# Spreading the adaLN gate's weight units evenly between the query projections of a hybrid attention kernel

## The reference

```python
def mixer_layer(x, c, pos, past, w_ada, b_ada, ln_gain, w_in, ...):
    mod = einsum('bd,de->be', silu(c), w_ada) + b_ada
    shift, scale, gate = split(mod, 3)
    h = rmsnorm(x, ln_gain) * (1 + scale) + shift
    q_a, ckv, krope, g_a, q_b, k_b, v_b, q_i, k_i, w_i, g_b = split(h @ w_in)
    # group A: latent attention over ckv, krope            -> o_a
    # group B: score = sum_g relu(q_i . k_i) * w_i ; top-k keys;
    #          softmax attention over them with a relative bias  -> o_b
    y = concat([rmsnorm(o_a) * silu(g_a), rmsnorm(o_b) * silu(g_b)])
    return x + gate * (y @ w_out)        # then a last rmsnorm
```

## Time and profile before

| | us |
|---|---|
| median of 3 runs | 999.13 (996.65 to 999.48) |
| the profiled execution's own time | 999.13 |
| its span in the profile | 997.3 |
| TensorE busy | 930.2 (93%) |
| TensorE's weight loads | 800.4 (80%) |
| VectorE busy | 428.0 (43%) |
| ScalarE busy | 340.7 (34%) |
| GpSimd busy | 116.9 (12%) |

### The profile page before, as it was taken

The page is one execution under the profiler, slowest core; times in us unless marked ns, Lnnn a source line. Parts: engine busy times, 40 slices in busy tenths (PEclk is TensorE's granted clock), DMA queues, the critical chain, the costliest instruction groups (busy, mean ns, idle before and its releaser), DMA issues.

```text
span 997.3 us, 14192 instructions
## 1 busy us (share of the span) xinstructions
PE 930.2 (93%) x5707; PEld 800.4 (80%) x5707; DVE 428.0 (43%) x882; ACT 340.7 (34%) x629; POOL 116.9 (12%) x189
## 2 busy tenths in 40 slices
PE   3798799999999999999999999998989999979996
PEld 0366478899999688888999889787978899868885
DVE  2221343336432145333333462349345566846462
ACT  2322342334311234223321542333134335632341
POOL 1000003102100000011103100102011101820000
PEclk9899899999999999999999999999999999999999
DMA  8999948665433234464324767547567753883423
GB/s 316 387 345 349 361 160 258 162 151 153 136 126 94 73 96 131 126 207 143 116 78 122 237 223 235 182 133 239 176 194 229 244 163 101 299 264 106 127 64 126
DMA packets 129537, 185.37 MB, mean 186 GB/s; under 512 B 30048, under 2 KB 79896, under 8 KB 128320
## 3 DMA queue, kind: packets, MB, share of 16 engines
q1 hardware_dynamic: 115744, 138.71, 44.3%
q0 software_dynamic: 13728, 45.76, 13.9%
HBM read 173.84 MB, written 12.69 MB: 187 GB/s over the span
## 4 chain that ended last, share of the span: by engine, by line
PE 80%; DMA 6%; DVE 5%; ACT 4%; issue 2%; SPq 2%; POOL 1%; DVEq 0%; ACTq 0%; POOLq 0%
PE proj L1736 30%; PE proj L1725 26%; DMA gl_b<-gate_scratch 3%; PE proj L1752 2%; DMA araw<-in_w_ada 2%; PE bankO L1709 2%; DVE w_lo L1276 2%; SPq L694 2%; PE bankO L1833 1%; PE bankO L1842 1%; PE proj L1709 1%; PE bankS L1752 1%; PE bankS L1959 1%; ACT w_hi L938 1%; DMA raw<-in_w_in 1%
## 5 line engine op out<-in xcount | busy, mean ns | idle before, releaser
L1276 DVE TENSOR_TENSOR w_lo<-raw,w_hi 128x1024 fp32r<-128x1024 f32 (+2 forms) x164 | 200.3, 1226 | 239.6 <-ACT w_hi L938 238.9
L938 ACT ACTIVATE w_hi<-raw 128x1024 fp32r<-128x1024 f32 (+2 forms) x164 | 167.7, 1026 | 191.0 <-PE proj L1725 101.5
L1736 PE MATMUL proj<-hT_hi,w_hi 128*128 128x384 f32 x640 | 222.2, 347 | 3.9 <-DVE w_lo L1276 2.8
L1736 PE MATMUL proj<-hT_hi,w_lo 128*128 128x384 f32 x640 | 215.1, 336 | 0.0
L1736 PE MATMUL proj<-hT_lo,w_hi 128*128 128x384 f32 x640 | 214.8, 336 | 0.0
L1725 PE MATMUL proj<-w_hi,hT_hi 128*128 128x512 f32 (+2 forms) x464 | 181.3, 391 | 16.0 <-DVE w_lo L1276 14.0
L1725 PE MATMUL proj<-w_hi,hT_lo 128*128 128x512 f32 (+2 forms) x464 | 176.3, 380 | 0.0
L1725 PE MATMUL proj<-w_lo,hT_hi 128*128 128x512 f32 (+2 forms) x464 | 176.0, 379 | 0.0
L1736 PEld LDWEIGHTS proj<-hT_hi,w_hi 128*128 128x128 f32 x640 | 121.0, 189 | 11.5 <-issue 7.2
L1736 PEld LDWEIGHTS proj<-hT_lo,w_hi 128*128 128x128 f32 x640 | 120.9, 189 | 0.5 <-issue 0.2
L1736 PEld LDWEIGHTS proj<-hT_hi,w_lo 128*128 128x128 f32 x640 | 120.6, 189 | 0.0
(11 more groups left out here) (350 smaller groups left out, 1043.5 us busy)
## 6 DMA issues: line engine op xcount, KB each, us to landing
raw<-in_w_in SPq DMA_DIRECT2D x104, 512.0 KB, 3.7
araw<-in_w_ada SPq DMA_DIRECT2D x128, 256.0 KB, 7.6
raw<-in_w_ada SPq DMA_DIRECT2D x32, 512.0 KB, 4.7
raw<-in_w_out SPq DMA_DIRECT2D x32, 512.0 KB, 3.9
raw<-in_w_in SPq DMA_DIRECT2D x32, 256.0 KB, 3.2
raw<-in_w_in SPq DMA_DIRECT2D x32, 128.0 KB, 2.6
wuk<-in_w_uk POOLq DMA_DIRECT2D x16, 256.0 KB, 3.8
kload<-in_cache_dsa_k POOLq DMA_DIRECT2D x8, 512.0 KB, 6.4
```

Of the source, the lines that this page charges most:

```text
L938: return nc.scalar.activation(out, in_, func, scale=scale, **kw)
L1276: V.tensor_tensor(w_lo[:, SLOT[u], 0:w], raw_of(u)[:, 0:w], high(u)[:, 0:w].bitcast(F32), ALU.subtract).then_inc(lo_ready, 1)
L1736: ins = mm(banks[blk][:, 0:TOK], w[:, n, cols], a[:, kt, :], start=first and n == m == 0, stop=final and n == per - 1 and m == 2)
```

## The change

In `units()`, one gate unit follows each dense unit of qi and qb. Before, two gate units followed every second one. So `d d g g d d g g` becomes `d g d g d g d g`, with the same units. The last unit of each chunk of qi and of qb is followed by one gate unit instead of two, so it stands one place later; its first unit stays. `plan()` isn't edited, but its rows are taken from these places.

```diff
--- before.py
+++ after.py
@@ -103,8 +103,8 @@
     gate = of("gate", 0) + of("gate", 1)
     for n, u in enumerate(dense):
         out.append(u)
-        if CHUNKS[u[0]][0] in ("qi", "qb") and u[1] % 2:
-            out += [gate.pop(0), gate.pop(0)]
+        if CHUNKS[u[0]][0] in ("qi", "qb"):
+            out.append(gate.pop(0))
     one, two = of("wo", 0), of("wo", 1)
     out += one[:4] + two[:4] + one[4:] + two[4:] + of("wo", 2) + of("wo", 3)
     return out
```

## The result

Median of 8 runs 1004.49 us (1002.30 to 1007.56) against 999.69 (995.88 to 1000.27) for the kernel before on the same chip. The ratio is 1.0057, 95% interval 1.0037 to 1.0077: about 5.7 us slower (the two means are 5.7 us apart, the two medians 4.8). The forecast was 1001.2 us and "the same"; 1004.5 lies inside the range of 8 in 10 and outside the forecast's own.

A forecast was written before the change was run, and what follows sets the result against it. TensorE, busy 93% of the span, was taken as the bound. The terms 2.3 + 0.57 - 1.1 - 0.2 + 1.05 + 2.8 - 3.4 made +2.0 us on 999.13: 1001.2 us, with 997.0 to 1005.0 for 8 in 10.

The forecast's parts named there:

- Step 1: More gate/dense switches: +2.3 us to the end of qi, +1.05 before gb, +0.57 for moved gate units.
- Step 2: TensorE's wait for the sum of squares (ysq) goes, covered by a dense unit: -1.1 us.
- Step 3: Top-k stretch: three waits of 1.2 to 1.3 us replace one of 2.8 and its slow clock: -0.2 us.
- (d): Rival: switches between kinds of matmul cost nothing, giving 997.8 us; chance 0.06.
- Step 4: First sample score: ld_kc 1 issued late, at t (end of qb's last dense unit) + 5.85: +2.8 us.
- rival (b): Load ld_kc 1 lands after 5.7 us, not 3.7: 2.0 us more, 1003.2 us; chance 0.10.
- Step 5: Sparse attention's ds to dv rows: same number of dense units, TensorE all but full: 0, give or take 1 us.
- Step 6: Output projection: dv 7's copy follows at once, -2.4 us; unit 242 starts earlier, -1.0; together -3.4.
- Rival (a): Output projection's give-back doesn't come, as transfers and weight loads set gl_b's landing: 1004.6 us; chance 0.22.

The follow-up runs named there:

- m1: a1 with ysq 0 put one row later; a single timed run of 997.86 us.
- d1: The kernel after (single gate units) with the sparse attention's rows put one back; 1.0032 of the kernel before.
- f1: The kernel before with gate units one by one in qb alone, pairs kept in qi; 1.0029 of the kernel before.
- g1: The kernel after with the load ld_kc 2 one row later; a single timed run of 1004.07 us.
- b1: The kernel before, its order of units kept, with the load ld_kc 1 one row later, behind gate 1's write-out; 1.0063 of the kernel before.
- a1: The kernel after with the load ld_kc 1 one row earlier, ahead of gate 1's write-out; 1.0006 of the kernel before.
- p1: c1 with yh 0 to 7 all one row later; a single timed run of 1001.37 us.
- c1: The kernel before, pairs kept, with ld_kc 1 issued early and the sparse attention's rows one later; 0.9981 of the kernel before.
- h1: The kernel before with y 14 and 15 one row later; a single timed run of 998.20 us.
- k1: The kernel before with yh 6 and 7 one row later; 0.9993 of the kernel before.
- r1: n1 with the first four loads of gl_b put two rows earlier; 0.9962 of the kernel before.
- n1: c1 with ysq 0 one row later; 0.9964 of the kernel before.
- e1: The kernel before with gate units one by one in qi alone, pairs kept in qb; 1.0034 of the kernel before.

## Why the prediction was wrong, step by step

- **Step 1, switches (+2.3, +0.57, +1.05): right.** In the chain after, a gate unit and a dense unit take 0.57 + 4.39 = 4.96 us, to the forecast's 4.94. With step 2 the stretch to ip 0 should have grown by 1.8 and grew by 3.0. Missed were 0.75 for w_lo (m1) and 0.21 for kic's bank, both new waits of under a microsecond; the last 0.3 is that two of each unit take 2 x 4.96 = 9.92 us against 9.53 before, 0.39 more and not 0.35. The last units ahead of gb cost 1.2, forecast 1.05. The rival that switches are free (d) falls with d1 and e1. The Trainium skill's page "TensorE: Matmul & The Clock Gate" ("Step-by-step: what each phase is for") has the next weights loaded while the running matmul streams, which would make a switch free; these runs don't agree, at 0.39 us for one pair of each kind that is split.
- **Step 2: right.** The 1.1 us is gone.
- **Step 3: right** in sum (-0.1, forecast -0.2), with waits of 1.43, 1.04 and 1.24 us where three of 1.2 to 1.3 stood in the text. That no slow clock follows them holds for this profile only (below).
- **Step 4: the mechanism right, two terms of it too small.** This is the step that failed. Forecast +2.8, measured +5.7 (f1 and g1, with the same steps there, +4.9 and +4.7). The load was issued 5.8 us behind t (forecast 5.85). Its landing was taken from the nearest row, 3.7, and was 5.3: +1.6, because, by the rows of f1, g1 and b1, a weight load went out with it; rival (b) had this at 5.7, with a chance of 0.10. The slow clock was taken as 1.5 and was 2.8: ks 1's eight transposes took 1.96 us and not 1.0, and the dense unit behind them 6.08 and not 4.2. This second term is not firm: behind waits of 4.0 and 4.2 us in the same place the dense unit took 5.35 us in f1 and 4.86 in g1, so the slow clock cost 2.1 and 1.6 us there. The longer wait doesn't explain it, and part of the 2.8 is the chance of this execution. The landing is firm, with 5.3, 5.25 and 5.5 us. That the load's place is the cause is shown both ways, by a1 and b1. The Trainium skill's page "DMA: Bandwidth & Descriptors" ("Anatomy of one DMA — SWDGE (gpsimd) path") gives an estimate of 3.2 us for such a load; b1's 3.72, with no weight load beside it, is 0.5 above it, and 5.3 and 5.5 beside one are not near it.
- **Step 5: wrong, +1.7 for 0.** "The same number of dense units" held, "all but full" did not. A wait of 1.4 us before dt 7 appears in every kernel with shifted rows, behind a w_lo of 2.07 us beside GpSimd's yh. In p1 it goes, a wait of 0.7 us for hT_lo comes in its place, and the stretch stays at 105.9. So the wait has its cause in where yh stands, but what makes up the 1.7 stays open.
- **Step 6: right in sign, -5.1 for -3.4, and its mechanism in part not what it said.** That yh 6 and 7 come ahead of dv 7 is the cause (c1 against p1). 1.0 by the order of y 14 and 15 holds (h1, and 2.4 against 3.4 us in all kernels with it). The other part was put to dv 7's copy and w_lo beside GpSimd; k1 shows that this alone is worth nothing, since GpSimd itself is then the late one. Rival (a), no give-back, falls, though its reason, transfers and weights on the same engines, may be part of how the gain comes about. The 1.7 us too much here cancel the 1.7 us too little of step 5, which is luck.
- **The tail, -0.8, not forecast.** TensorE's wait before unit 242 is 4.8 us and not 5.85 or the forecast 6.5, and the half clock behind it shorter (906.0 to 909.8 after, 894.2 to 901.0 before). Between kernels with the same work there this stretch took 99.0 to 101.8 us, so 0.8 is within what executions differ by.

The sum: 3.0 - 0.1 + 1.2 + 5.7 + 1.7 - 5.1 - 0.8 = +5.6, for +2.0.

## What to carry to other kernels

When an order of work is moved by one place, look on each queue for the steps that now stand behind a wait that they stood ahead of: here one load behind one store cost as much as the whole change did in net, and moving it back cost nothing. Price such a load not by its quietest landing but by one with the same neighbours, and add the half clock behind the wait as a range (1.6 to 2.8 us here behind waits of 4.0 to 4.2). A gain that rests on a copy or a load coming sooner should be tried by itself before it is believed, since the next thing on the same queue may be as late.

## What the runs showed of the hardware

The half clock behind one and the same wait is not the same from one execution to the next. Behind a wait of 2.7 to 2.8 us the same 48 matmuls took, in the chains of r1, h1, n1 and c1:

```profile
693.18 8.61 PE proj L1736 x48
```

```profile
694.74 10.17 PE proj L1736 x48
```

```profile
696.21 10.19 PE proj L1736 x48
```

```profile
692.65 11.37 PE proj L1736 x48
```

So 0.1, 1.6, 1.7 and 2.8 us above the 8.53 of the earlier trace rows. Up to this point h1, c1 and the kernel before (10.18) are the same program, and so are n1 and r1. Behind the wait of 1.4 us for kl 1's bank, 24 matmuls took in the chains of a1 and d1

```profile
677.04 4.17 PE proj L1736 x24
```

```profile
680.13 5.75 PE proj L1736 x24
```

The queue in the output projection differs too: from the issue of the four loads to yh 12 it took 36.1 to 39.7 us in the five profiles with the steps of before there (before, b1, d1, e1, h1) and 38.7 to 39.9 in the eight with those of after. The largest difference lies ahead of everything that was changed: unit 150 starts at 535.7 us in a1 and at 542.7 in the kernel after. Runs of the kernel before spread over 8 us (993.64 to 1001.92, 29 of them on one chip). A term of 1.6 us read from a single profile is therefore one throw of several.
